# Moving the roots of the next block's norm behind the last two weight splits, and x to ScalarE's queue

## The reference

```python
def even_layer(x, norm_g, w_in, conv_w, pool_w, pool_scale, w_out):
    h = rmsnorm(x, norm_g)
    xa, bg, cg, gate_a, u, gate_b = split_cols(h @ w_in, EVEN_SIZES)
    ya = short_conv_mixer(xa, bg, cg, conv_w) * jax.nn.silu(gate_a)
    yb = pool_mixer(u, pool_w, pool_scale) * jax.nn.silu(gate_b)
    return x + jnp.concatenate([ya, yb], axis=-1) @ w_out

def odd_layer(x, norm_g, w_in, i_bias, f_bias, sinks, w_out):
    h = rmsnorm(x, norm_g)
    ...                                # attention (window 128) and mLSTM on slices of h @ w_in
    return x + jnp.concatenate([yc, yd], axis=-1) @ w_out

# rmsnorm(x, g) = x * rsqrt(mean(x*x) + 1e-6) * g ; after both layers: rmsnorm(x, final_norm)
```

## Time and profile before

| what | value |
|---|---|
| median of 3 runs | 1854.32 us (1851.87 to 1855.83) |
| profiled execution, its own time | 1854.15 us |
| its span, first to last instruction | 1852.3 us |
| mean granted TensorE clock | 0.967 of 2.4 GHz |
| TensorE busy | 1743.7 us (94%) |
| VectorE, ScalarE, GpSimd busy | 53%, 22%, 53% |
| chain that ended last | PE 83%, issue 5%, POOL 5%, DVE 4% |
| DMA | mean 90 GB/s |

### The profile page before, as it was taken

One profiled execution on the slowest core, in us unless ns is written; L12 is line 12 of the kernel. 1 busy time (PEld: TensorE's weight loads), 2 busy tenths in 40 slices (PEclk: granted clock), 3 DMA queues, 4 the chain that ended last, 5 costly groups with the idle time before them and its releaser, 6 DMA issues.

```text
span 1852.3 us, 23603 instructions
## 1 busy us (share of the span) xinstructions
PE 1743.7 (94%) x8512; PEld 1445.7 (78%) x8512; DVE 982.4 (53%) x1392; ACT 406.0 (22%) x997; POOL 987.3 (53%) x655
## 2 busy tenths in 40 slices
PE   6999899997999989999799998999979998999995
PEld 4888678886888867888688886888868876788884
DVE  4556336754656425574374632667447573256734
ACT  2001123322100013332210112333220001233321
POOL 6666454345666655334566655533556666444352
PEclk8999899998999989999899998999989999999997
DMA  5332243213433224322343322432224322242231
GB/s 166 94 99 92 57 96 87 69 58 114 138 96 98 91 57 97 75 69 66 116 139 92 92 91 69 95 77 58 87 96 145 95 91 80 69 103 69 58 125 46
DMA packets 252426, 167.15 MB, mean 90 GB/s; under 512 B 41968, under 2 KB 226800, under 8 KB 252304
## 3 DMA queue, kind: packets, MB, share of 16 engines
q1 hardware_dynamic: 232640, 148.92, 28.1%
q10 hardware_dynamic: 19664, 16.63, 3.2%
HBM read 157.07 MB, written 8.45 MB: 89 GB/s over the span
## 4 chain that ended last, share of the span: by engine, by line
PE 83%; issue 5%; POOL 5%; DVE 4%; ACT 2%; ACTq 1%; DMA 0%; POOLq 0%; DVEq 0%
PE bank L425 12%; PE bank L427 11%; PE bank L426 11%; PE pair_a L425 5%; PE pair_a L426 5%; PE pair_a L427 5%; PE pair_b L425 4%; PE pair_b L426 4%; PE pair_b L427 4%; PE pair_c L425 3%; PE pair_c L426 3%; PE pair_c L427 3%; PE pair_a L680 3%; POOL w_lo L416 2%; PE pair_c L664 2%
## 5 line engine op out<-in xcount | busy, mean ns | idle before, releaser
L414 POOL TENSOR_SCALAR w_hi<-stage 128x1024 fp32r<-128x1024 f32 x264 | 289.6, 1097 | 740.7 <-PE bank L427 468.3
L416 POOL TENSOR_TENSOR w_lo<-stage,w_hi 128x1024 fp32r<-128x1024 f32 x264 | 660.4, 2502 | 22.0
L425 PE MATMUL bank<-h_hi,w_hi 128*128 128x512 f32 x960 | 380.3, 396 | 1.5 <-DVE h_lo L995 1.5
L427 PE MATMUL bank<-h_hi,w_lo 128*128 128x512 f32 x960 | 375.6, 391 | 0.0
L426 PE MATMUL bank<-h_lo,w_hi 128*128 128x512 f32 x960 | 375.0, 391 | 0.0
L425 PEld LDWEIGHTS bank<-h_hi,w_hi 128*128 128x128 f32 x960 | 181.2, 189 | 38.6 <-issue 2.9
L427 PEld LDWEIGHTS bank<-h_hi,w_lo 128*128 128x128 f32 x960 | 180.8, 188 | 38.6
L426 PEld LDWEIGHTS bank<-h_lo,w_hi 128*128 128x128 f32 x960 | 181.2, 189 | 36.5 <-issue 1.0
L425 PE MATMUL pair_a<-h_hi,w_hi 128*128 128x512 f32 x256 | 101.7, 397 | 0.8 <-POOL w_lo L416 0.8
L926 ACT ACTIVATE work<-work,sm 128x256 f32<-128x256 f32 x128 | 63.6, 498 | 168.7 <-DVE sm L1263 168.7
L427 PE MATMUL pair_a<-h_hi,w_lo 128*128 128x512 f32 x256 | 99.7, 389 | 0.0
(11 more groups left out here) (282 smaller groups left out, 3401.8 us busy)
## 6 DMA issues: line engine op xcount, KB each, us to landing
stage<-in_even_w_in SPq DMA_DIRECT2D x96, 512.0 KB, 3.7
stage<-in_odd_w_in SPq DMA_DIRECT2D x88, 512.0 KB, 3.8
stage<-in_even_w_out SPq DMA_DIRECT2D x32, 512.0 KB, 3.7
stage<-in_odd_w_out SPq DMA_DIRECT2D x32, 512.0 KB, 3.8
xin<-in_x SPq DMA_DIRECT2D x20, 512.0 KB, 5.7
stage<-in_odd_w_in SPq DMA_DIRECT2D x32, 256.0 KB, 4.7
result<-res ACTq DMA_DIRECT2D x16, 512.0 KB, 3.9
work<-gate_rows ACTq DMA_DIRECT2D x16, 256.0 KB, 5.0
```

What stands on the lines that cost most here:

```text
L414: g.tensor_scalar(w_hi[sl][:, :], stage[sg][:, :], 1.0, 0.0, ALU.mult, ALU.add).then_inc(s_whi, 1)
L416: g.tensor_tensor(w_lo[sl][:, :], stage[sg][:, :], w_hi[sl][:, :].bitcast(F32), ALU.subtract).then_inc(s_split, 1)
L425: t.matmul(dst, l_hi, r_hi, start=start, stop=False)
L427: return t.matmul(dst, l_lo, r_hi, start=False, stop=stop)
```

## The change

On SyncE the request of x is removed. On ScalarE it stands between the `y_hi` copies and the squares, with the same wait. On GpSimd the four roots no longer stand ahead of the split of unit 63: roots 0 and 1 stand behind the split of unit 64, roots 2 and 3 behind the split of unit 65. The programs of TensorE and VectorE are unchanged.

```diff
@@ SyncE: loop over units
                     sp.wait_ge(s_split, b * UNITS + i + 1)
                     load_unit(i)
-                    if i == U_OOUT + 4:
-                        sp.wait_ge(s_yo, b * 8 + 8)
-                        load_x(((b + 1) % NB) * TB)
@@ GpSimd: loop over units
-                    if i == U_OOUT + 5:
-                        for tt in range(TT):
-                            pool.wait_ge(s_first, b * 5 + TT + 2 + tt)
-                            root_of(b * 8 + 2 * TT + tt, 0, tt, b * 24 + 16 + 2 * tt + 2)
...
                     g.tensor_tensor(w_lo[sl][:, :], stage[sg][:, :], w_hi[sl][:, :].bitcast(F32),
                                     ALU.subtract).then_inc(s_split, 1)
+                    if i >= U_OOUT + 6:
+                        for tt in ((0, 1), (2, 3))[i - U_OOUT - 6]:
+                            pool.wait_ge(s_first, b * 5 + TT + 2 + tt)
+                            root_of(b * 8 + 2 * TT + tt, 0, tt, b * 24 + 16 + 2 * tt + 2)
@@ ScalarE: behind the y_hi copies
+                act.wait_ge(s_yo, b * 8 + 8)
+                for tt in range(TT):
+                    act.dma_start(xin[:, tt, :], x[0][bass.ds(((b + 1) % NB) * TB + tt * P, P), :]
+                                  ).then_inc(s_x[tt], 16)
                 for tt in range(TT):
                     act.wait_ge(s_x[tt], b * 16 + 32)
```

## The result

| what | before | changed |
|---|---|---|
| median | 1854.84 us (1851.87 to 1855.83) | 1872.82 us (1870.96 to 1874.28) |
| profiled execution / its span | 1854.15 / 1852.3 us | 1871.43 / 1869.6 us |
| TensorE busy | 1743.7 us | 1751.9 us |
| mean granted clock | 0.967 | 0.972 |

Four runs each; the ratio is 1.0099, 95% interval 1.0082 to 1.0117. The kernel is slower by 18.0 us; 24.6 were forecast. The lines of the changed kernel are numbered a few lower than before: L405 and L407 are the splits, L385 and L387 a root, L434 the transposes, L420 to L422 the three passes, L986 the scale, L953 the request of x.

A forecast was written before the change was run, and what follows sets the result against it. TensorE's own work plus its stops bound the kernel. From unit 62's end to unit 64's, new terms sum to 31.72 us against 25.57: +6.15 a block, +24.6 over four, 1854.3 + 24.6 = 1879 us; range 1868 to 1889.

The forecast's parts named there:

- The 9.6 us wait goes: TensorE before unit 63: split 63 waits for unit 61 alone, ready near 446, so the 9.6 us wait goes.
- First new wait 6.07 us: TensorE after unit 62, before tile 0's transposes: split 64, root, scale and transposes in a chain, 6.07 us a block.
- Tile 1 and its transposes: Before unit 63: root 1 waits for VectorE's sum behind scale 0, 2.36 us; eight transposes at 1.2 GHz, 1.56.
- Unit 63, 6.8 us: Unit 63 starts without a wait, part of the slow stretch perhaps over: 6.8 us, between 5.55 and 7.74.
- rival B: Each stop pays the whole slow stretch: units 63 and 64 take 7.74 each, +7.5 us a block, 1884 us; chance 20%.
- Second wait 6.07, transposes 1.56, unit 64 7.3: After unit 63: tile 2's root stands behind split 65, 6.07 us; transposes 1.56, then unit 64 at 7.3.
- Tile 3 and all that follows cost nothing: After tile 2: scale to scale, 3.55 us, fits inside unit 64; nothing later shifts against TensorE.
- x from ScalarE's queue is worth nothing: Request of x moved from SyncE to ScalarE: value 0, a later x covered by more than 8 us.
- A: Clock stays high through both 6 us stops, units 63 and 64 at 5.55: +1.6 us a block, 1861 us; chance 7%.
- E: Units 63 and 64 both as slow as block 3's 8.46: +9.0 us a block, 1890 us; more than 1889, chance 8%.
- C: Only the first wait comes; tile 2's root is ready when unit 63 ends: -2.4 us a block, 1844.6 us; chance 3%.
- D: Nothing changes: lost and found time cancel within 0.9 us a block, 1854 us; chance 2%.

The follow-up runs named there:

- second wait alone: Kernel before with roots 0 and 1 left ahead of split 63, roots 2 and 3 moved behind split 65, x on SyncE's queue: 1843.22 us, ratio 0.9948.

## Why the prediction was right, and where its size was off

- **The 9.6 us wait goes, split 63 is ready before unit 62 ends.** Right: 445.22, forecast near 446.
- **First new wait 6.07 us.** 5.98, 5.98, 5.98 and 5.99. The chain was put together from durations that each had a row (0.36 + 3.52 + 0.86 + 1.28 + 0.05), and it came out within 0.1. The undisturbed 2.39 us for `w_lo` was the right choice too: the two moved splits took 2.34.
- **Tile 1 and its transposes, 2.36 + 1.56 = 3.92.** 3.89, 4.00, 4.00, 3.99.
- **Unit 63, 6.8 us.** This is the term that was mis-sized. It took 5.63 on the mean, 1.17 less, 4.7 us over four blocks. That alone is a little more than the 4.4 by which the stretch fell short of 24.6; the other terms give 0.3 back. I had weighed two answers, that the transposes and their four microseconds bring the clock back in part, and that they do nothing (rival B, 7.74), and had taken a value between. When unit 63 starts, the clock is all but back. Over the changed kernel and the three experiments that have the first wait and unit 63 behind it (roots alone moved, all roots behind split 64, extra transposes behind unit 63), sixteen blocks, thirteen took 5.55 to 5.85, two 6.1 and one 6.87; in the kernel before and with x alone moved, where unit 63 follows the stop directly, eight blocks took 7.02 to 8.46. That transposes count is shown by the 72 extra ones, which held the clock.
  But they need not have shortened the slow stretch. Counted from the moment TensorE starts again, 1.2 GHz lasted 3.1 to 6.3 us in the kernel before, where unit 63 itself is the first work. It lasted 3.8 to 4.3 us at unit 63 of the changed kernel, where all but 0.3 at most lie ahead of the unit, and 5.4 to 5.7 at its unit 64, where 1.6 lie ahead; with the second wait alone 3.3 to 4.9, with the roots alone moved 6.7 in the one slow block (all worked out from lengths and granted clocks of windows). So the slow stretch is not shorter behind the transposes than without them; the transposes stand in it, and less of it is left for the unit. The expensive part of a slow stretch is what falls on the unit's matmuls. No run separates the number of transposes from the time that they take, and why the slow stretch varies from 3.1 to 6.7 us, no run shows.
- **Second wait 6.07, transposes 1.56, unit 64 7.3.** 5.98, 1.62 and 7.42 on the mean: 0.3 us less, 0.2 and 0.5 more over four blocks. The 7.3 was a value taken between bounds like the 6.8, and that it came out this close is luck: with the second wait alone the same unit took 6.4 to 7.1.
- **Tile 3 and all that follows cost nothing.** Right: tile 3's transposes begin at unit 64's end in each block.
- **x from ScalarE's queue is worth nothing.** Right, to 0.1% (x alone moved). It did not land sooner; it landed 1.5 us later in block 0 (0.7 to 2.2 over the blocks), inside a cover of eight. The Trainium skill (DMA: Bandwidth & Descriptors, Issuing engines are not separate DMA queues) says that requests of all engines run on the same 16 DMA engines, so that another issuer saves only issue time. The runs agree in that nothing was gained (ratio 0.9999), and here not even issue time was saved: four requests took 1.95 us on ScalarE and 1.96 on SyncE. That the engines are shared, no run here shows.
- **The sum.** Stretch +20.2 us for +24.6, time +18.0 us. The remaining 2 us are less than the spread of the rest of the kernel between executions (1745.6 to 1750.2 us).
- **The rivals.** A (the clock stays high) fell: the clock was down after both stops. Only A's length of unit 63 came true, and by another way, the clock being back in time. B (7.74 for both units) fell for unit 63 and came near for unit 64 (7.42); E (8.46) fell for both. C (no second wait) fell in the changed kernel; with the roots so placed that the second wait is gone (all behind split 64), the kernel took 1840.4 us for the 1844.6 worked out. D fell. The mean clock I had said would be below 0.967; the profiled execution had 0.972. That sign was badly chosen: runs of one and the same kernel differ by 0.008 in it, more than the change is worth.

The two waits, taken from the best version one at a time: first alone 1840.4, second alone 1843.2, neither 1811.0. So the waits cost 29.4 and 32.2 us, 61.6 together; the changed kernel, which has both, is 61.8 above the best. They add up as far as the runs can tell: each median is good to some 1 to 2 us, so the 0.2 between the sums is luck, and by the four stretches of each profile the waits cost 27.5 and 31.9 against 61.5 for both. Each price holds the slow stretch behind the wait.

## What to carry to other kernels

A small producer must not stand behind a large task that waits for the consumer to finish: put the two tiny root instructions behind a split that is released by the end of a unit, and the consumer pays split, root and scale in a row, at each such place. Ask of each position in an engine's program what releases the instruction ahead of it, and when; the best of the orders run here is neither the one before nor the change, but two roots ahead of split 63 and two behind split 64, which runs while TensorE is busy with unit 63 (43 us faster). And price a stop of TensorE with the slow stretch behind it: 1.5 to 2.9 us at unit 63 of the kernel before, 1.8 to 1.9 at unit 64 of the changed one. Ask what work comes first behind the stop: it is that work which runs slowly.

## What the runs showed of the hardware that was not expected

- Float32 transposes of 128 x 128 alone, one each 0.11 us, held the granted clock at 1.00 for 8.9 us; without them it fell to 0.50 there in the kernel before (452.00 to 458.69, no matmul). Filling TensorE's waits with work that nobody reads made the kernel before 9.3 us faster and the changed one 9.6 us (8.4 by the ratios).
- Behind a 6.0 us stop and sixteen transposes spread over four microseconds, the following unit took 5.55 to 5.85 us in 13 of 16 blocks. Behind the same stop and eight transposes done in 1.6 us, it took 6.4 to 7.5 us in all twelve blocks that have them (the changed kernel, the roots alone moved, the second wait alone).
- The request of 2 MB of x and the load of 0.5 MB of weights beside each other: the first tile of x came 1.5 us later in block 0 (0.7 to 2.2 over the blocks) than when the weights waited behind it.
